# Where GpSimd asks for the last cached values, who stores the second group's statistics, and a second probability tile

## The reference

```
h = x * (1 + scale) + shift;  proj = h @ w_in
mixer A: three groups of 4 heads attend with (window, dilation) = (128,1), (512,4), (2048,16);
         the groups are combined by the softmax denominators (the statistics)
mixer B: gated DeltaNet, 6 heads, d = 128, exact delta rule in chunks:
         (I + strict_lower(beta k k^T * decay)) u = beta v ...   a triangular system for each chunk
merged = sigmoid(..) * branch_a + sigmoid(..) * branch_b;  x = LayerNorm(alpha * x + gate * merged @ w_o)
```

## Time and profile before

| | |
|---|---|
| median of 3 runs | 2397.6 us (2394.88 to 2401.76) |
| profiled execution: own time, span | 2393.71 us, 2391.9 us |
| TensorE busy | 2283.3 us (95%) |
| VectorE busy | 1633.2 us (68%) |
| ScalarE busy | 1164.7 us (49%) |
| GpSimd busy | 373.0 us (16%) |
| DMA | 363.56 MB, mean 152 GB/s |
| `vc` loads | 8, 1152.0 KB each, median 10.3 us to land |
| `kc` loads | 8, 1152.0 KB each, median 11.6 us to land |

### The profile page before, as it was taken

One profiled execution on the slowest core, in us unless ns is written; L12 is line 12 of the kernel. 1 busy time (PEld: TensorE's weight loads), 2 busy tenths in 40 slices (PEclk: granted clock), 3 DMA queues, 4 the chain that ended last, 5 costly groups with the idle time before them and its releaser, 6 DMA issues. The chain is left out here.

```text
span 2391.9 us, 45040 instructions
## 1 busy us (share of the span) xinstructions
PE 2283.3 (95%) x16842; PEld 2043.8 (85%) x16842; DVE 1633.2 (68%) x4012; ACT 1164.7 (49%) x2453; POOL 373.0 (16%) x628
## 2 busy tenths in 40 slices
PE   5999999999999999999999989879998899999998
PEld 2778788888899999999999978658887699999786
DVE  5877776555363676776645559659987877777897
ACT  4444444444421454444444468647776533333554
POOL 0000000000111011110000001123321034445100
PEclk7999999999999999999999999979999699999999
DMA  7232323332532233223333367975665556567563
GB/s 270 97 115 97 115 98 115 106 106 88 189 121 75 93 104 121 86 102 111 111 110 102 109 253 238 340 205 161 156 178 186 190 176 216 182 194 238 190 213 124
DMA packets 258249, 363.56 MB, mean 152 GB/s; under 512 B 56934, under 2 KB 192718, under 8 KB 253552
## 3 DMA queue, kind: packets, MB, share of 16 engines
q1 hardware_dynamic: 199456, 224.11, 30.4%
q0 software_dynamic: 36560, 125.17, 13.7%
q10 hardware_dynamic: 22016, 11.40, 1.7%
HBM read 246.94 MB, written 113.68 MB: 151 GB/s over the span
## 5 line engine op out<-in xcount | busy, mean ns | idle before, releaser
L320 PE MATMUL ps_f<-m_lo,w_hi 128*128 128x272 f32 (+1 forms) x2436 | 788.4, 324 | 13.4 <-DVE m_lo L648 6.8
L320 PE MATMUL ps_f<-m_hi,w_hi 128*128 128x272 f32 (+1 forms) x2436 | 793.6, 326 | 0.0
L320 PE MATMUL ps_f<-m_hi,w_lo 128*128 128x272 f32 (+1 forms) x2436 | 784.7, 322 | 0.0
L320 PEld LDWEIGHTS ps_f<-m_lo,w_hi 128*128 128x128 f32 x2436 | 458.9, 188 | 54.1 <-issue 17.8
L320 PEld LDWEIGHTS ps_f<-m_hi,w_lo 128*128 128x128 f32 x2436 | 459.6, 189 | 36.9
L320 PEld LDWEIGHTS ps_f<-m_hi,w_hi 128*128 128x128 f32 x2436 | 458.8, 188 | 33.7
L712 DVE TENSOR_TENSOR stage<-partial,ps_f 128x512 f32<-128x512 f32 (+2 forms) x348 | 183.6, 544 | 308.3 <-PE ps_f L320 298.7
L453 ACT ACTIVATE partial<-ps_f 128x272 f32<-128x272 f32 (+1 forms) x348 | 160.7, 462 | 374.6 <-PE ps_f L320 373.2
L415 ACT ACTIVATE w_hi<-w_raw 128x512 fp32r<-128x512 f32 x348 | 212.6, 625 | 195.3 <-PE ps_f L320 113.7
L619 DVE TENSOR_TENSOR w_lo<-w_raw,w_hi 128x512 fp32r<-128x512 f32 x348 | 239.2, 688 | 84.5 <-ACT w_hi L415 80.6
L738 DVE SCALAR_TENSOR_TENSOR conv<-stage,side,conv 128x1024 f32<-128x1024 f32 x108 | 138.4, 1281 | 8.3 <-ACT conv L469 7.0
(11 more groups left out here) (775 smaller groups left out, 4707.3 us busy)
## 6 DMA issues: line engine op xcount, KB each, us to landing
w_raw<-in_w_feat SPq DMA_DIRECT2D x58, 1024.0 KB, 5.7
gates<-scratch_g_d SPq DMA_DIRECT2D x56, 256.0 KB, 3.4
m_rows<-scratch_parts_d SPq DMA_DIRECT2D x16, 768.0 KB, 4.8
z_f<-scratch_z_d ACTq DMA_DIRECT2D x13, 768.0 KB, 6.4
scratch_conv_d<-conv POOLq DMA_DIRECT2D x18, 544.0 KB, 3.0
scratch_conv_d<-conv POOLq DMA_DIRECT2D x18, 512.0 KB, 2.9
kc<-in_k_cache SPq DMA_DIRECT2D x8, 1152.0 KB, 11.6
vc<-in_v_cache POOLq DMA_DIRECT2D x8, 1152.0 KB, 10.3
```

What stands on the lines that cost most here:

```text
L320: last = pe.matmul(out[:, 0:n], l[:, cols], r, start=start and k == 0 and nth == 0, stop=k == KH - 1 and nth == 2, skip_group_check=not start)
```

## The change

Four things are changed.

- The four DMAs with the second group's statistics leave SP's list and stand in GpSimd's, behind its multiplications for `q_bd`, with a semaphore of their own. The values of the second and third group share the semaphore of their keys, so scores wait for both.
- The samples' probabilities get a tile for each half. The small tiles `top`, `neg`, `den` and `rden` become columns of one tile `few`.
- `decay_sums(1)` and `decays(1)` move in front: on TensorE ahead of the second half's scores, on ScalarE ahead of the copies. ScalarE copies the turned probabilities of both halves; VectorE's `turned` is gone.
- The loads of `vc` for sequences 4 to 7 are asked for after GpSimd's reload of the first system.

```diff
-        v_in = [sem(f"v_in{g}") for g in range(NG)]
+        v_in = [sem("v_in0")] + qk_in[1:]
...
-        stats_stored = sem("stats_stored")
-        late.update(rows_out=row_stored, stats_out=stats_stored, prompt_scored=s_full[1], prompt_weighed=o_full)
+        stats_stored, stats1_stored = sem("stats_stored"), sem("stats1_stored")
+        late.update(rows_out=row_stored, stats_out=stats_stored, stats1_out=stats1_stored, prompt_scored=s_full[1], prompt_weighed=o_full)
...
-                store_stats(1)
...
-                elif g == 1:
-                    for j in range(4):
-                        sp.dma_start(st[512 * j:512 * (j + 1)].rearrange("(m s) n -> m s n", s=step), stats[:, g, j::4]).then_inc(stats_stored, 16)
...
                                            DH ** -0.5, None, ALU.mult).then_inc(late["put"], 1)
+            pool.wait_ge(stat_put, 2 * NBLK)
+            for p in range(NP_):
+                pool.wait_ge(exp_done[p], 4 * NBLK)
+            for j in range(4):
+                pool.dma_start(t["stats_d"][512 * j:512 * (j + 1), 1, :].rearrange("(m s) n -> m s n", s=GROUPS[1][1]), stats[:, 1, j::4]).then_inc(stats1_stored, 16)

...
-                    pe.wait_ge(qk_in[x.g], (128, 80)[x.g - 1])
+                    pe.wait_ge(qk_in[x.g], (128 + 64, 80 + 16)[x.g - 1])
...
-                    pe.wait_ge(v_in[x.g], (64, 16)[x.g - 1])
+                    pe.wait_ge(v_in[x.g], (128 + 64, 80 + 16)[x.g - 1])
...
-        probs = sb("probs_s", [P, KEYS])
+        probs = [sb(f"probs_s{a}", [P, KEYS]) for a in range(2)]
         probs_T = sb("probs_T_s", [P, KT_C, P])
         new_T = sb("new_T_s", [SAMP, NG, P])
-        top = sb("top_s", [P, len(BANKS)])
-        neg = sb("neg_s", [P, 1])
-        den = sb("den_s", [P, 2])
-        rden = sb("rden_s", [P, 2])
+        few = sb("few_s", [P, 2, 8])
+        top, neg, den, rden = few[:, :, 0:len(BANKS)], few[:, :, 3], few[:, :, 4], few[:, :, 5]
...
             pool.dma_start(t["G_rows"].rearrange("b (h p) -> (b h) p", p=P), G_row[:, :]).then_inc(row_out, 16)
-            pool.wait_ge(late["stats_out"], 16 * 6)
+            pool.wait_ge(late["stats_out"], 16 * 2)
+            pool.wait_ge(late["stats1_out"], 16 * 4)
             for g in range(NG):
                 pool.wait_ge(late["rows_out"][g], 16 * 4)
-            values(4, 5, 6, 7)
             for c in range(2):
...
             pool.dma_start(pair["sub_u"][NSUB // 2:], system_of(t, 0)).then_inc(pair["sub_in"][1], 16)
+            values(4, 5, 6, 7)
             pool.wait_ge(pair["causal_in"], 16)
...
-                            last = pe.transpose(ps_t[u % 2][0:SAMP, g, :], probs[:, P + SAMP * g:P + SAMP * (g + 1)], ident[:, :])
+                            last = pe.transpose(ps_t[u % 2][0:SAMP, g, :], probs[a][:, P + SAMP * g:P + SAMP * (g + 1)], ident[:, :])
                     else:
                         for n, k in enumerate(tiles):
-                            last = pe.transpose(ps_t[u % 2][:, n, :], probs[:, col[k]:col[k] + P], ident[:, :])
+                            last = pe.transpose(ps_t[u % 2][:, n, :], probs[a][:, col[k]:col[k] + P], ident[:, :])
...
                     if c and h == 4:
-                        pe.wait_ge(t_read, len(ROUNDS))
+                        pe.wait_ge(row_put, 1)
                     pe.matmul(place_of_G(c, h), g_c[:, c, h:h + 1].broadcast_to([P, P]), tri[:, 0, :], start=True, stop=False)
...
             score_cached(0)
-            decay_sums(0)
+            decay_sums(0), decay_sums(1)
             pe.wait_ge(maxed, 1)
             score_new(1), score_cached(1)
+            pe.wait_ge(E_done, 2)
             turn(0)
-            pe.wait_ge(t_read, len(ROUNDS) - 1)
-            decay_sums(1)
             grams(0), grams(1)
-            pe.wait_ge(E_done, 2)
             weigh(0)
...
-                if a:
-                    dve.wait_ge(t_full, len(ROUNDS))
                 at = 0
                 for b, w in enumerate(BANKS):
-                    ins = dve.tensor_tensor_reduce(out=probs[:, at:at + w], in0=ps_s[b][:, 0:w], in1=bias[:, a, at:at + w],
+                    ins = dve.tensor_tensor_reduce(out=probs[a][:, at:at + w], in0=ps_s[b][:, 0:w], in1=bias[:, a, at:at + w],
                                                    scale=1.0, scalar=-3.0e38, op0=ALU.add, op1=ALU.max,
-                                                   accum_out=top[:, b:b + 1])
+                                                   accum_out=top[:, a, b:b + 1])
                     at += w
                     if b < len(BANKS) - 1:
                         link(ins)
                 ins.then_inc(maxed, 1)
                 dve.wait_ge(maxed, a + 1)
-                dve.tensor_reduce(neg[:, :], top[:, :], AX.X, ALU.max, negate=True).then_inc(neg_done, 1)
+                dve.tensor_reduce(neg[:, a:a + 1], top[:, a, :], AX.X, ALU.max, negate=True).then_inc(neg_done, 1)

             def shares(a):
                 dve.wait_ge(exped, a + 1)
                 dve.reciprocal(rden[:, a:a + 1], den[:, a:a + 1]).then_inc(softened, 1)
-
-            def turned():
-                for r, tiles in enumerate(ROUNDS):
-                    dve.wait_ge(t_full, r + 1)
-                    src = ps_t[r % 2]
-                    if tiles == "new":
-                        ins = dve.tensor_copy(new_T[:, :, :], src[0:SAMP, 0:NG, :])
-                    else:
-                        ins = dve.tensor_copy(probs_T[:, tiles[0]:tiles[-1] + 1, :], src[:, 0:len(tiles), :])
-                    ins.then_inc(t_read, 1)
...
-            turned()
...
-                act.activation(probs[:, :], probs[:, :], ACT.Exp, bias=neg[:, :], accum_out=den[:, a:a + 1]).then_inc(exped, 1)
+                act.activation(probs[a][:, :], probs[a][:, :], ACT.Exp, bias=neg[:, a:a + 1], accum_out=den[:, a:a + 1]).then_inc(exped, 1)
...
-            def turned():
+            def turned(a):
                 for r, tiles in enumerate(ROUNDS):
-                    u = len(ROUNDS) + r
+                    u = len(ROUNDS) * a + r
...
-            decays(0)
+            decays(0), decays(1)
+            turned(0)
             exps(1)
-            decays(1)
             act.wait_ge(row_out, 16)
             for b in range(2, 4):
                 act.dma_start(G_in[:, b % 2].rearrange("p h n -> p (h n)"), t["G_rows"][b].partition_broadcast(P)).then_inc(pair["G_loaded"][b % 2], 16)
             outputs(0)
-            turned()
+            turned(1)
```

## The result

The changed kernel took 2403.39 us (median of 20 runs, 2395.02 to 2409.15), the kernel before, timed beside it on the same chip, 2394.35 us (20 runs, 2384.3 to 2401.76). The ratio is 1.0035, 95% interval 1.0026 to 1.0044: slower by 8.4 us. (The ratio is worked out from all runs and not from the two medians, which lie 9.0 us apart.) The forecast of 2394.6 us, 3.0 us of gain, was wrong, and its range, up to 2402.0, did not hold the time. Its base, the median 2397.6 of three runs, lay 3.2 us above that of the 20, so the time was missed by less (8.8 us) than the change (11.4 us).

What follows compares the result with a forecast made beforehand. TensorE, busy 95% of the span, bounds the kernel, so only its stalls or slow clock can yield time. Masks -1.6 us and clock -1.4 us give 3.0 us off the median 2397.6: 2394.6 us, range 2388.5 to 2402.

Steps and rivals of the forecast that it cites:

- `vc` asked for at 1552.4: GpSimd's queue: the moved `vc` loads are issued behind the first system's reload, 9.5 us later than before.
- elimination's end 1572.6: VectorE: first system's elimination begins 9.3 us earlier, at 1557.3, and so ends at 1572.6.
- weighting 1568.0: Second half's weighting starts when `vc` lands, 6.9 us later than 1561.09, and becomes last in place of the elimination.
- masks' end 1585.5: VectorE's masks: weighting at 1568.0 plus 11.2 to first gram plus 6.3; before 1587.1, so -1.6 us.
- the clock's gain of 1.4 us: TensorE between masks and first product: two sets of key transposes at the higher clock, 0.7 us off each.
- The landing 15.6 us behind the first issue: `vc` loads: issue at 1552.4 plus 16.6, less 1.9 for `G_first`, plus 0.9 for SP's rows, landing at 1568.0.
- SP's rows: SP's six loads in 512-byte rows, sharing packets one for one with `vc`, were to cost it about 0.9 us.
- Rival 1: SP's six loads take their full bytes, 5.8 us, ahead of `vc`: +3.3 us, 2400.9 on the median; chance 0.17.
- Step 1: SP's solution store at 1582.3 leaves VectorE's turned diagonal at 1590.6, capping the gain at 3.0 us.
- rival 3: Gain goes nowhere: first product waits for something counted as covered, or the clock drops; -1.2 to +1; chance 0.20.
- Step 2: Loop over block pairs, TensorE and VectorE nearly full: the first product's 3.0 us shift carries to the end.
- Step 3: Second group's statistics on GpSimd's queue: the earlier wait now stands before the masked blocks; gain by itself 0.

Runs made afterwards that it cites:

- e3: Changed kernel with the four `vc` loads asked for ahead of the first system's stores again: 2388.96 us, ratio 0.9984 to the kernel before.
- e13: Changed kernel with all six of SP's loads (`xkq`, `xv`) held until `vc` has landed: 2401.03 us, ratio 1.0022 to the kernel before.
- e11: Changed kernel with only SP's two `xv` loads held until `vc` has landed: 2400.58 us, ratio 1.0026 to the kernel before.
- e4: Kernel before with only the four `vc` loads moved behind the first system's reload: 2402.38 us, ratio 1.0034 to the kernel before.
- e5: Changed kernel with the solution's store ahead of the wait for the second half's outputs: 2393.82 us, ratio 0.9989 to the kernel before.
- e10: Changed kernel with three `vc` loads ahead of the stores, one behind the reload, and the solution's store in front: 2390.8 us, ratio 0.9992 to the kernel before.
- e2: Changed kernel, unedited, traced and timed a second time: 2399.01 us, ratio 1.0017 to the kernel before.
- e6: Kernel before with only the second group's statistics stored by GpSimd: 2391.34 us, ratio 0.998 to the kernel before.
- e8: Changed kernel with two `vc` loads ahead of the first system's stores and two behind its reload: 2396.52 us, ratio 1.0001 to the kernel before.
- e9: Changed kernel with two `vc` loads ahead of the stores, two behind the reload, and the solution's store in front: 2389.89 us, ratio 0.9976 to the kernel before.

## Why the prediction was wrong

*What held.* In the time of before, as forecast and as measured in the three traces: `vc` asked for at 1552.4, 1551.7; elimination's end 1572.6, 1572.7; weighting 1568.0, 1568.6 to 1569.5; masks' end 1585.5, 1585.4 to 1585.9. Two of these agree by luck. The elimination starts at 1556.0, 1.3 us earlier than forecast, and takes 16.7 us in place of 15.4, since GpSimd's additions of 1557.81 now fall into it: its first instruction took 1.53 us in place of 0.19 and ended with them. The masks hide a weighting 0.6 to 1.5 us late behind a stretch from weighting to grams of 10.4 us in place of 11.2. Also as forecast was the clock's gain of 1.4 us between masks and product, seen as 0.87 us for six key transposes and as 5.1 us from masks to product in e3, against 5.0. The landing 15.6 us behind the first issue was mis-sized (16.9 to 17.7), which an issue 0.7 us earlier hid. SP's rows were given 0.9 us of it, one for one, and cost about 1.7 by e13; the rest I put down to their head start up to 1559.5, which no run separates. Rival 1, which gave them their full 5.8 us, is refuted by e11 and e13.

*Step 1 that failed: "from SP's solution store at 1582.00 ... 1582.3. So the diagonal does not get earlier, and it stops the gain at 3.0 us."* The store was issued where forecast, at 1582.6 to 1583.0. But I let it land in the 2 us of before, without asking what stands ahead of it: the two `xv` loads of 0.79 MB, which before had been issued 7.6 us earlier, at 1574.41, now 1.1 us earlier. It took 5.4 us to land. Over all 16 traces the landing goes with the distance to the first of those loads: 5.3 to 6.1 us where it was issued 1.1 us ahead (six traces), 4.1 us at 2.4 us (e4), and 2.0 to 2.3 us at 3.8 us or more, or with the loads behind (nine). So the diagonal came 4 us late and took the whole gain: product at 1593.5 to 1594.1 against 1593.6 and 1592.7. This is what rival 3 names in half a sentence ("the solution's store behind it"), priced there at -1.2 to +1. e5 shows it: with the store in front, it lands in 2.0 us, the first product is 2.8 us earlier, and weighting and masks do not move.

*Step 2 that failed: "a shift of this first product is a shift of the end."* Of the 7.4 us between the forecast's -3.0 and the traces' end at +4.4, 3.7 are there at the first product and 3.0 at chunk 0; the others come behind it.

Chunk 1 is 1.3 us behind, where chunk 0 was level. SP's list also holds the reload of the second system and, behind it, the loads of `G_first`, all about 4 us later now (1594.3 against 1590.57 for the reload). The second elimination does not start later for it (1601.3 to 1601.5, against 1601.9 and 1601.0), but it takes longer: its first 76 instructions took 11.9 to 12.2 us in place of 10.2. GpSimd's additions, which wait for `G_first`, now fall into it. Of the changed kernel, then of before:

```profile
1606.24 1.80 POOL L2382 TENSOR_TENSOR ET_first<-G_first,causal_T 128x768 f32<-128x768 f32 x1 [1.17 <-DMA G_first<-scratch_G_rows]
1606.26 1.93 DVE L1039 TENSOR_TENSOR sub_prod<-sub_u,sub_w 96x29 f32<-96x29 f32 x2
```
```profile
1602.77 0.29 DVE L1039 TENSOR_TENSOR sub_prod<-sub_u,sub_w 96x29 f32<-96x29 f32 x2
```

VectorE's pair took 1.93 us in place of 0.29 and ended with GpSimd's addition. In the five traces with no addition in this stretch it takes 10.2 us, in the other eleven 10.8 to 13.1, the more the longer the two overlap (0.7 to 3.2 us). The state's update stands behind these 76 instructions and comes 1.5 us later.

From chunk 12 to 13 another 2.3 us go. By the table that step is 14.0 to 14.8 us in five traces and 16.5 or more in the other eleven. The granted clock divides them the same way: it stays at 1.00 in the five, and is at 0.50 for 3.4 us of the step in ten and for 6.8 us in e10. TensorE waits once in the step, for the state from VectorE. In before, then in the changed kernel, with its clock:

```profile
1804.37 1.60 PE L2543 MATMUL ps_c<-S,xkq 128*128 128x128 f32 x12 [1.56 <-DVE S L2705]
```
```profile
1810.24 2.93 PE L2528 MATMUL ps_c<-S,xkq 128*128 128x128 f32 x12 [2.92 <-DVE S L2690]
1810.00:1813.00 3.00, 2.75 (x12) 2.63 (x12) 3.00 (x22) 1.86 (x6) 0.00 (x0) 0.50 0.00 0
```

The wait is 2.92, 2.17 and 2.71 us against 1.56 and 2.01, 0.8 us more: the last system's elimination starts 7.5, 7.0 and 7.6 us behind GpSimd's issue of its reload, against 6.3 and 6.7 before. From the end of the wait to chunk 13 it is 8.1 us in each of the five traces and 9.5 to 9.7 in the ten, 1.5 us more for the clock, and 11.0 in e10. Why the clock falls in the eleven stays open: waits of 2.17 us stand on both sides (e5 at 1.00, e2 at 0.50). The last 0.7 us, behind chunk 13, are not placed.

*Step 3, not an error of the sum but of the question: statistics, "Gain by itself: 0".* It was right for the change as made, since the wait that became shorter no longer had the loads behind it. It hid that the earlier end of this wait was the change's one gain: with the loads left in place it is worth 4 to 5 us (e3, e6). I priced the move of the loads against the kernel before instead of against the kernel with the other edits.

*The clock.* My sum has it only between masks and first product. The long stretch at the lower level in e4, e8 and e13, 5 us up to chunk 0, is in none of the three traces of the changed kernel. Its timed runs have the lower mean clock told above, but where in the span they lose it is not on record.

## What to carry to other kernels

A queue is a list twice over: of issues that wait for each other, and of bytes that land in order. When a wait in such a list becomes later, ask for each DMA behind it what now stands directly ahead of it, and give it the landing time of a row with the same neighbours, not of the same DMA. A large load should be asked for as early as its buffer allows; whether in pieces, so that small transfers on a dependent chain slip between them, is suggested by e9 but not shown, since all four ahead with the store in front was not run. And an edit that moves it is priced against the version with all other edits, one at a time.

## What was not expected of the hardware

- A reload of 192 KB issued directly behind four loads of 4.72 MB on the same queue landed after 16.9 us; issued directly ahead of them it took 4.8 us.
- The store of 192 KB took 5.4 us behind two loads of 384 KB just issued on its queue, 2.0 us with 7.6 us between.
- While GpSimd ran an addition of 128 x 768 values (1.80 us), two small instructions of VectorE took 1.93 us in place of 0.29, and 76 of them 10.8 to 13.1 us in place of 10.2.
- The same code ran with TensorE busy for 9.3 of 10 us at 1.00 and for 10.0 of 10 us at 0.50, and took 15.5 to 16.7 us or 20.9 us (e4, e8, e13) from the product to chunk 0.
- All that lies ahead of the prompt's attention took up to 6.7 us more or less from one execution to the next (shifts of -2.55 to +4.14 us): of a trace only what follows a common place can be compared to the microsecond.
